# Two early weight slabs, grouped means, a final norm in token layout, and four unread matmuls in the MLP's norm

## What is computed

```python
    x = x + rmsnorm(merged @ w_o, norm_mix_post)       # end of the mixer: phase "wo"
    h = rmsnorm(x, norm_mlp_pre)                        # the MLP's norm
    f = jnp.square(jax.nn.relu(h @ w_up)) @ w_down      # phases up0..up3, down0..down3
    x = x + rmsnorm(f, norm_mlp_post)
...
    x = x + (silu(h @ w_ffn_gate) * (h @ w_ffn_up)) @ w_ffn_down   # fup*, fdown0..fdown2
    return x * rsqrt(mean(x * x, axis=-1) + EPS) * norm_final      # the final norm
```

## Time and profile before

| | us |
|---|---|
| median of three runs | 1579.6 (1579.47 to 1580.46) |
| the profiled execution: its time | 1579.75 |
| the profiled execution: its span | 1577.8 |
| PE busy / DVE / ACT / POOL | 1490.5 (94%) / 788.6 (50%) / 505.8 (32%) / 156.2 (10%) |
| mean granted TensorE clock | 0.978 of full |
| line 402, all products of `gemm` | 68% of the chain that ended last |

### The profile page before, as it was taken

How to read it: one execution, slowest core, us unless ns; L and a number is a source line. 1 busy time by engine, 2 the same in 40 slices (tenths; PEclk the granted TensorE clock), 3 DMA queues, 4 the chain that set the end, 5 groups by cost and what they waited for, 6 DMA issues and landing times.

```text
span 1577.8 us, 16902 instructions
## 1 busy us (share of the span) xinstructions
PE 1490.5 (94%) x7062; PEld 1202.7 (76%) x7062; DVE 788.6 (50%) x1011; ACT 505.8 (32%) x668; POOL 156.2 (10%) x114
## 2 busy tenths in 40 slices
PE   4999989799999999879989899999998999999997
PEld 3888768578888888648777587777886888888885
DVE  5999663544234343463683745455435433433433
ACT  4222343443332322244443333332233222212212
POOL 0040013000000000200240211110220000000001
PEclk9999999899999999989999999999998999999998
DMA  5332213122233232412331021010222323233221
GB/s 150 107 107 95 80 66 107 54 81 94 93 107 97 91 107 81 147 60 81 81 80 56 27 65 44 3 51 10 84 94 80 95 93 107 80 107 107 81 80 54
DMA packets 138136, 129.52 MB, mean 82 GB/s; under 512 B 14581, under 2 KB 134636, under 8 KB 138060
## 3 DMA queue, kind: packets, MB, share of 16 engines
q1 hardware_dynamic: 135552, 124.27, 25.2%
q0 software_dynamic: 992, 3.47, 0.7%
q10 hardware_dynamic: 1516, 0.69, 0.2%
HBM read 126.32 MB, written 2.10 MB: 81 GB/s over the span
## 4 chain that ended last, share of the span: by engine, by line
PE 88%; DVE 7%; ACT 2%; issue 2%; DMA 1%; POOL 0%; ACTq 0%; DVEq 0%; POOLq 0%
PE gemm L402 68%; PE gemm L773 4%; PE gemm L511 2%; PE misc L800 2%; PE misc L785 2%; PE gemm L428 1%; PE misc L793 1%; PE gemm L543 1%; PE misc L786 1%; DVE rstd L1306 1%; DMA conv_rows<-in_conv_w 1%; DVE w_lo L1297 1%; DVE q_level L1623 1%; PE misc L628 1%; ACT w_hi L879 1%
## 5 line engine op out<-in xcount | busy, mean ns | idle before, releaser
L402 PE MATMUL gemm<-h_hi,w_hi 128*128 128x512 f32 x1136 | 446.4, 393 | 5.2 <-DVE w_lo L1297 5.2
L402 PE MATMUL gemm<-h_lo,w_hi 128*128 128x512 f32 x1136 | 443.3, 390 | 0.0
L402 PE MATMUL gemm<-h_hi,w_lo 128*128 128x512 f32 x1136 | 443.2, 390 | 0.0
L1297 DVE TENSOR_TENSOR w_lo<-w_raw,w_hi 128x2048 fp32r<-128x2048 f32 (+1 forms) x111 | 251.4, 2265 | 190.7 <-ACT w_hi L879 190.6
L879 ACT ACTIVATE w_hi<-w_raw 128x2048 fp32r<-128x2048 f32 (+1 forms) x115 | 216.8, 1885 | 145.8 <-PE gemm L402 138.1
L402 PEld LDWEIGHTS gemm<-h_hi,w_hi 128*128 128x128 f32 x1136 | 214.2, 189 | 54.5 <-DVE w_lo L1297 6.3
L402 PEld LDWEIGHTS gemm<-h_hi,w_lo 128*128 128x128 f32 x1136 | 214.0, 188 | 44.6
L402 PEld LDWEIGHTS gemm<-h_lo,w_hi 128*128 128x128 f32 x1136 | 214.0, 188 | 44.6 <-issue 0.5
L402 PE MATMUL gemm<-f_hi,w_hi 128*128 128x512 f32 x432 | 168.0, 389 | 0.0
L402 PE MATMUL gemm<-f_lo,w_hi 128*128 128x512 f32 x432 | 168.0, 389 | 0.0
L402 PE MATMUL gemm<-f_hi,w_lo 128*128 128x512 f32 x432 | 168.0, 389 | 0.0
(11 more groups left out here) (329 smaller groups left out, 1658.8 us busy)
## 6 DMA issues: line engine op xcount, KB each, us to landing
w_raw<-in_w_in SPq DMA_DIRECT2D x62, 512.0 KB, 4.6
w_raw<-in_w_down SPq DMA_DIRECT2D x32, 512.0 KB, 4.1
w_raw<-in_w_up SPq DMA_DIRECT2D x30, 512.0 KB, 4.6
w_raw<-in_w_ffn_gate SPq DMA_DIRECT2D x22, 512.0 KB, 4.4
w_raw<-in_w_ffn_up SPq DMA_DIRECT2D x22, 512.0 KB, 4.7
w_raw<-in_w_ffn_down SPq DMA_DIRECT2D x16, 512.0 KB, 4.0
w_raw<-in_w_o SPq DMA_DIRECT2D x8, 512.0 KB, 4.5
w_raw<-in_w_out SPq DMA_DIRECT2D x8, 512.0 KB, 4.1
```

Source lines behind the costliest of these rows:

```text
L402: mm = nc.tensor.matmul(bank[:], w[s % RING][:, kt, col0:col0 + P], x(n), start=first, stop=last)
L1297: V.tensor_tensor(part(lo_of(s), s), part(raw_of(s), s), f(part(hi_of(s), s)), SUB).then_inc(S("lo_done"), 1)
```

## The change

- **Two early slabs.** `EARLY` holds the second and the third slab of `up0`; each has raw, high and low buffers of its own, the low part being written over the raw one. SP issues both loads right after that of the first slab, once the blocks before `wo` are done; they have semaphores of their own. ScalarE splits both at block 6 of `wo`, after its regular split and ahead of that block's evacuation; VectorE makes both low parts at the end of `wo`.
- **Grouped means.** In `first_up` the means of the eight squares no longer stand between the products but behind them all, and the spread of the roots comes after the low products of the first of the four blocks.
- **Unread matmuls.** `keep_busy(n)` runs n products `INV` x `SQA` of 128 x 512 in plain float32 into bank `M[3]`, which nobody reads. One stands behind the mean of `SQA`, one behind the mean of the last square, two behind the spread.
- **The final norm in token layout.** ScalarE writes x times the gain, `XG`, for tiles 0 to 6 during `fdown2`, VectorE for tile 7. The sum of squares is used as the weight operand against one column of `INV`, so that the means land as 128 x 4, one token per partition. Root and reciprocal are 128 x 4. The transposes take `XG`, unscaled; the factor of the norm is applied when the transposed tile is read from PSUM, on VectorE for tiles 0, 2, 4, 6, 7 and on ScalarE (four instructions each) for 1, 3, 5. The eight tiles use eight banks in turn instead of four.

```diff
-    UPRAW, UPHI, UPLO = at("up_raw", [KT, SLAB], f32, R1 + 32), at("up_hi", [KT, SLAB], f32r, R1 + 40), at("up_lo", [KT, SLAB], f32r, R1 + 48)
+    UPRAW = [at(f"up_raw{i}", [KT, SLAB], f32, R1 + 32 + 16 * i) for i in range(2)]
+    UPLO = [at(f"up_lo{i}", [KT, SLAB], f32r, R1 + 32 + 16 * i) for i in range(2)]
+    UPHI = [at(f"up_hi{i}", [KT, SLAB], f32r, R1 + 40 + 16 * i) for i in range(2)]
...
-    SECOND_UP = PH["up0"][0] + 1
+    EARLY = {PH["up0"][0] + 1: 0, PH["up0"][0] + 2: 1}
...
+    XG = at("x_gained", [KT, T], f32, 16)
+    ROOT_TOK, RSTD_TOK = at("out_root", [TT], f32, SB + 12), at("out_rstd", [TT], f32, SB + 12.5)
+    OUT_BANKS = M[0:3] + [G[(PH["fdown2"][2] + k) % 4] for k in (7, 4, 5, 6)] + M[0:1]
+    DVE_TILES, ACT_TILES = (0, 2, 4, 6, 7), (1, 3, 5)
...
@@ SP, load() @@
+            if s in EARLY:
+                sp.wait_ge(S("block_full"), PH["wo"][2])
+                for dst, src in pieces:
+                    sp.dma_start(dst, src).then_inc(S(f"up_raw_ready{EARLY[s]}"), 16)
+                return
             if s >= RING:
                 sp.wait_ge(S("lo_done"), s - 1)
-            if s == SECOND_UP:
-                sp.wait_ge(S("block_full"), PH["wo"][2])
...
@@ TensorE, the norm @@
+        def keep_busy(n):
+            for _ in range(n):
+                nc.tensor.matmul(M[3][:], INV[1024][:], SQA[:], start=True, stop=True)
         pe.wait_ge(S("sq_added"), KT)
         mean_rows(SQA[:], True, False)
+        keep_busy(1)
         pe.wait_ge(S("wo_squared"), KT)
         mean_rows(SQ[1][:], False, True).then_inc(S("mean_ready"), 1)
+        keep_busy(1)
         spread_rstd(M[1], 1)
+        keep_busy(2)
...
@@ TensorE, first_up(), behind the loop's products @@
-                for e in {0: (), 6: (5, 6, 7), 7: ()}.get(k, (k - 1,)):
-                    pe.wait_ge(S("x1_squared"), e + 1)
-                    mm = mean_rows(Y[:, e, :], e == 0, e == KT - 1)
-                    if e == KT - 1:
-                        mm.then_inc(S("mean_ready"), 1)
-            spread_rstd(M[2], 2)
+            for k in range(KT):
+                pe.wait_ge(S("x1_squared"), k + 1)
+                mm = mean_rows(Y[:, k, :], k == 0, k == KT - 1)
+            mm.then_inc(S("mean_ready"), 1)
             for b in range(4):
+                if b == 1:
+                    spread_rstd(M[2], 2)
...
@@ TensorE, the end @@
-        mean_of_sum(3, (S("ysq_ready"), 3 * KT))
-        for k in range(KT):
-            pe.wait_ge(S("hs_ready"), 3 * KT + k + 1)
-            if k >= 4:
-                pe.wait_ge(S("out_ready"), k - 3)
-            bank = M[k % 4]
+        def out_tile(k):
+            pe.wait_ge(S("x_gained"), k + 1)
             for t in range(TT):
-                mm = nc.tensor.transpose(bank[:, t * P:(t + 1) * P], HS[k % 2][:, t * P:(t + 1) * P], IDENT[:])
+                mm = nc.tensor.transpose(OUT_BANKS[k][:, t * P:(t + 1) * P], XG[:, k, t * P:(t + 1) * P], IDENT[:])
             mm.then_inc(S("out_T"), 1)
+        b0 = PH["fdown2"][2]
+        pe.wait_ge(S("sq_added"), 4 * KT)
+        for t in range(TT):
+            nc.tensor.matmul(M[3][:, t:t + 1], SQA[:, t * P:(t + 1) * P], INV[1024][:, 0:1], start=t == 0, stop=False)
+        out_tile(0)
+        out_tile(1)
+        pe.wait_ge(S("ysq_ready"), 3 * KT)
+        for t in range(TT):
+            mm = nc.tensor.matmul(M[3][:, t:t + 1], SQ[1][:, t * P:(t + 1) * P], INV[1024][:, 0:1], start=False, stop=t == TT - 1)
+        mm.then_inc(S("mean_ready"), 1)
+        out_tile(2)
+        pe.wait_ge(*evac_at(b0 + KT - 1))
+        for k in range(3, 7):
+            out_tile(k)
+        pe.wait_ge(S("out_ready"), 1)
+        out_tile(7)
...
@@ ScalarE, wo @@
+            if k == KT - 2:
+                split_hi(s0 + 5)
+                split_hi(s0 + 6)
             if k == KT - 1:
-                split_hi(SECOND_UP)
                 nc.scalar.activation(TMP16[:, 0:1], EPSB[:], ACT.Sqrt)
...
@@ ScalarE, the end (each k of fdown2, then the tiles) @@
+            if k == KT - 1:
+                A_(TMP16[:, 0:1], EPSB[:], ACT.Sqrt)
+            last(k, b0 + k, 0)
+            if k < KT - 1:
+                A_(XG[:, k, :], XT[:, k, :], ACT.Copy, scale=col("norm_final_2", k)).then_inc(S("x_gained"), 1)
+        act.wait_ge(S("mean_ready"), 7)
+        A_(ROOT_TOK[:], M[3][:, 0:TT], ACT.Sqrt, bias=EPSB[:]).then_inc(S("out_rooted"), 1)
+        act.wait_ge(S("out_inverted"), 1)
+        for k in ACT_TILES:
             act.wait_ge(S("out_T"), k + 1)
+            for t in range(TT):
+                ins = A_(OTK[:, t, k * P:(k + 1) * P], OUT_BANKS[k][:, t * P:(t + 1) * P], ACT.Copy, scale=RSTD_TOK[:, t:t + 1])
+            ins.then_inc(S("odd_out_ready"), 1)
...
@@ VectorE, wo and the end @@
-        split_lo(SECOND_UP)
+        for s in EARLY:
+            split_lo(s)
...
-        invert(6, (S("hs_ready"), 3 * KT))
+        dve.wait_ge(*evac_at(b0 + KT - 1))
+        dve.wait_ge(S("x_gained"), KT - 1)
+        V.tensor_scalar(XG[:, KT - 1, :], XT[:, KT - 1, :], col("norm_final_2", KT - 1), None, MUL).then_inc(S("x_gained"), 1)
+        dve.wait_ge(S("out_rooted"), 1)
+        V.reciprocal(RSTD_TOK[:], ROOT_TOK[:]).then_inc(S("out_inverted"), 1)
+        dve.wait_ge(S("out_inverted"), 1)
+        for k in DVE_TILES:
+            dve.wait_ge(S("out_T"), k + 1)
+            V.tensor_tensor(OTK[:, :, k * P:(k + 1) * P], OUT_BANKS[k][:].rearrange("p (t d) -> p t d", d=P),
+                            RSTD_TOK[:].unsqueeze(2).broadcast_to([P, TT, P]), MUL).then_inc(S("out_ready"), 1)
```

More of the change, by code:

```diff
@@ L206, in raw_full @@
     def raw_full(s):
-        return raw_ready[s % RING], 16 * sum(PIECES[s % RING:s + 1:RING])
+        if s in EARLY:
+            return S(f"up_raw_ready{EARLY[s]}"), 32
+        return raw_ready[s % RING], 16 * sum(PIECES[x] for x in range(s % RING, s + 1, RING) if x not in EARLY)
     def wide(t):
@@ L215, in evac_at @@
         return evac[m % 4], m // 4 + 2 + i * (per // 4)
-    SECOND_UP = PH["up0"][0] + 1
+    EARLY = {PH["up0"][0] + 1: 0, PH["up0"][0] + 2: 1}
     def raw_of(s):
-        return UPRAW if s == SECOND_UP else RAW[s % RING]
+        return UPRAW[EARLY[s]] if s in EARLY else RAW[s % RING]
     def hi_of(s):
-        return UPHI if s == SECOND_UP else WHI[s % RING]
+        return UPHI[EARLY[s]] if s in EARLY else WHI[s % RING]
     def lo_of(s):
-        return UPLO if s == SECOND_UP else WLO[s % RING]
+        return UPLO[EARLY[s]] if s in EARLY else WLO[s % RING]
     def part(t, s):
@@ L382, in _ @@
         for k in range(KT):
-            sp.wait_ge(S("out_ready"), k + 1)
+            if k in DVE_TILES:
+                sp.wait_ge(S("out_ready"), DVE_TILES.index(k) + 1)
+            else:
+                sp.wait_ge(S("odd_out_ready"), ACT_TILES.index(k) + 1)
             sp.dma_start(out[0].rearrange("(t p) c -> p t c", p=P)[:, :, k * P:(k + 1) * P],
@@ L399, in gemm @@
                     ready(n)
-                for w, x in ((WHI, hi), (WHI, lo), (WLO, hi)):
-                    last = n == len(kts) - 1 and w is WLO
-                    mm = nc.tensor.matmul(bank[:], w[s % RING][:, kt, col0:col0 + P], x(n), start=first, stop=last)
+                for w, x in ((hi_of, hi), (hi_of, lo), (lo_of, hi)):
+                    last = n == len(kts) - 1 and w is lo_of
+                    mm = nc.tensor.matmul(bank[:], w(s)[:, kt, col0:col0 + P], x(n), start=first, stop=last)
                     first = False
@@ L876, in split_hi @@
                 act.wait_ge(*raw_full(s))
-                if s >= RING:
+                if s >= RING and s not in EARLY:
                     act.wait_ge(S("block_full"), BLOCKS_BEFORE[s - 1])
@@ L906, in run @@
                 for j in range(2):
-                    if s0 + 2 * i + j + 1 != SECOND_UP:
+                    if s0 + 2 * i + j + 1 not in EARLY:
                         split_hi(s0 + 2 * i + j + 1)
@@ L1268, in _ @@
         last = x_square(3 * KT)
[L1269 to L1274, removed]
-        for k in range(KT):
+        for k in range(KT):
+            if k % 2 == 0:
+                split_hi(s0 + k // 2 + 1)
+            if k == KT - 1:
[7 more added lines that the diff above has]
+        for k in ACT_TILES:
             act.wait_ge(S("out_T"), k + 1)
-            A_(OTK[:, :, k * P:(k + 1) * P], M[k % 4][:].rearrange("p (t d) -> p t d", d=P), ACT.Copy).then_inc(S("out_ready"), 1)
+            for t in range(TT):
+                ins = A_(OTK[:, t, k * P:(k + 1) * P], OUT_BANKS[k][:, t * P:(t + 1) * P], ACT.Copy, scale=RSTD_TOK[:, t:t + 1])
+            ins.then_inc(S("odd_out_ready"), 1)
     @block.vector
@@ L1336, in run @@
                 for j in range(2):
-                    if s0 + j + 1 + 2 * i != SECOND_UP:
+                    if s0 + j + 1 + 2 * i not in EARLY:
                         split_lo(s0 + j + 1 + 2 * i)
```

## The result

The changed kernel takes 1567.9 us (median of four runs, 1566.2 to 1568.9) against 1580.0 us for the kernel before in the same comparison (1579.5 to 1581.6): ratio 0.992, 95% interval 0.990 to 0.994. That is 12.1 us less. The prediction said 1561.5, with a range of 1559.3 to 1564.8, so 18.1 less. The profiled execution has a span of 1566.7 us and took 1568.7.

The account below looks back on a forecast made before the run. TensorE bounds the kernel, carrying 88% of the span, so only its waits and low-clock stretches can win. The norm's 12.5 us and the end's 5.6 sum to 18.1 less, giving 1561.5 us, range 1559.3 to 1564.8.

Parts of the forecast that it names:

- (a) to (g): The steps for the MLP's norm between `wo` and `up0`: in sum, the third slab comes 12.5 us earlier.
- rival B: The fourth slab of `up0` takes over the third's wait, stopping TensorE 1 to 3 us: 1564.5 us, chance 0.08.
- (b): MLP's norm: the first unread product costs 0.5 us, leaving the last square's mean 2.9 us earlier in all.
- (c): MLP's norm: if the clock stays up, spreading the roots costs 0.89 us and not 2.09, 1.2 gained.
- rival A: Unread products don't hold the clock in the MLP's norm: 2.1 to 3.4 us more, taken as 1564.0, chance 0.13.
- Part 2, the end: Final norm: the first tile and with it the kernel's end come earlier, 5.6 us gained, bounds 4.8 and 6.6.
- the term for gaps between stores: Stores at the kernel's end: about 0.1 us of gaps between them goes.
- The sum over the whole: Whole kernel: 12.5 + 5.6 = 18.1 us less, so 1561.5 us, chance 0.63.
- clock changes elsewhere: Stages outside the two changed places: an allowance of 0.7 us in the range, at its low end of 1559.3.
- rival D: The shift makes the attention stage, 936 to 1096, lose the clock for half its 160 us: 1601.5 us, chance 0.03.
- The rule weighed against the rows: MLP's norm: no gap left is long enough for a fall, so 1561.5 stays; one row showed a fall regardless.

Follow-up runs that it names:

- the filled kernel: The changed kernel with unread products also in TensorE's other long waits, and one wait at the start moved forward and lengthened: 1555.1 us, ratio 0.984.
- the shorter product: The filled kernel with the first unread product of the norm cut to 256 columns: 1556.9 us, ratio 0.986.
- the second comparison: The changed kernel run again unaltered, against the kernel before at 1580.6 us: 1566.6 us, ratio 0.991.

## Why the prediction was wrong, and where it was right

- **(a) to (g), the norm: right as a sum, in part by luck.** 12.5 us forecast, 12.4 measured (46.6 to 34.3 us between the same products). The first product of `up0` came 0.5 us later than forecast (7.8 and not 7.3 us after the last one of `wo`), for the two reasons below; from there to the third slab it took 24.9 instead of 25.3, which gives most of it back. The other parts hold: the third slab without a wait, means in one group 1.88 (forecast 2.1 with the changes of kind), the 64 high products 14.77 (14.8). The fourth slab didn't take over the wait, so rival B is out.
- **(b), the first unread product: undersized.** From the start of `wo`'s last product to the mean of the last square it is 1.84 us in the filled kernel, 1.42 with the shorter product, 1.07 without. So it costs 0.77, not 0.5; with that the last square's mean comes 2.6 us earlier than before, not 2.9.
- **(c), the clock: right as to the fact; the price of a fall lay in rival A's range, but in other places.** The clock held in the norm of all executions profiled with the four products. Without them the norm took 1.8 to 2.0 us more, although the 0.77 of the first product were saved, so the fall itself cost 2.5 to 2.8; rival A had 2.1 to 3.4. All of it lies in the 64 high products, 17.24 and 17.50 us instead of 14.77. The 1.2 that rival A charged for the spread didn't come: in the run without them the spread was over before the clock fell at 291.4. And the 1.2 that (c) counts as won by a quick spread was 0.9, since at full clock the spread takes 1.17 us here (the row at 291.31) and not the 0.89 of the row at 317.89.
- **Part 2, the end: right, a little small.** 5.6 forecast, 6.2 measured (19.5 to 13.3, also with this part alone). The first store came 3.9 us after the end of the blocks, as worked out. What was too small is the term for gaps between stores: from the first store's tile to the end it is 9.2 instead of 9.75, so 0.5 and not 0.1.
- **The sum over the whole: wrong.** The step that failed is the one that carried 18.1 us from the two places to the end of the kernel. It took everything behind the norm as moved but unchanged, with 0.7 us "for clock changes elsewhere" in the range. Measured, the second part took 3.9 to 5.6 us more in the three executions profiled with the new norm and nothing altered behind it, with 10 to 14 us more at 1.2 GHz; a delay of 1.29 us gave the kernel before the same 5.6, and one of 2.14 us took them from the changed kernel. The mechanism was named in rival D, that the clock's decisions are not tied to the kernel's start, but with the wrong place, the attention stage, with a price of 40 us instead of 5, and with a chance of 0.03. The argument against it there, that runs of the kernel before lie within 1 us, was read the wrong way round. The falls of one and the same kernel lie at the same distances from its instructions although the executions start differently, so their agreement says nothing of what another place against the clock's decisions costs.
- The rest of the gap in medians, 12.1 measured against 18.1, is most likely chance: in the comparison of the result the profiled execution also lost 1.9 us ahead of the change. In the second comparison the difference is 14.0, which agrees with the 18.5 of the two places less 3.9 to 5.6.
- **The rule weighed against the rows.** The Trainium skill ("TensorE: Matmul & The Clock Gate", "Why this matters for your kernels") ties a fall to idle gaps longer than those left in the norm; with the four products the clock held, as it says. The falls of the changed kernel at 918 and of the filled one at 906 came while the profile shows TensorE busy without a gap, and a rule on gaps doesn't cover them.

Left open: why the clock falls at some of the later places and not at others. And that a late execution catches up half at each half-speed stretch is an explanation that fits the profiles; it wasn't tested by itself.

## What to carry to other kernels

A gain in one place moves all that follows against the clock's own decisions. If later stages have waits in which the clock can fall, count for each the products behind the wait at both speeds, and take the sum as the uncertainty of the forecast, even where repeated runs agree closely. Pure delays of one or two us, where TensorE never waits, show whether a missing gain went there. Take more than one, and compare the profiles part by part: here 1.71 us brought back only half, and what 2.14 us won over all hardly rose above the noise. Better than looking for a good place is to leave the clock few occasions: unread products in most of the long waits were worth 11.5 us here, nearly as much as the change itself.

## What the runs showed of the hardware that was not expected

A fall with TensorE busy throughout, in the filled kernel, among products of 31 columns:

```profile
903.00:906.00 3.00, 3.00 (x46) 2.60 (x44) 1.67 (x8) 0.00 (x0) 0.00 (x0) 0.93 0.00 0
906.00:909.00 3.00, 3.00 (x26) 2.84 (x24) 0.50 (x1) 0.00 (x0) 0.00 (x0) 0.50 0.00 0
```

A busy time of 3.00 of 3 us in the profile doesn't mean that the clock is safe. And a delay can shorten what comes after it: with 2.14 us of unread work the second part took 922.8 instead of 926.7 and 928.4 us.
